# The opening of a two-layer backbone kernel: the first modulation group computed by halves

## The reference, cut to what matters

```python
def reference(x, c, ctx, c_ctx, w_mod, b_mod, g_pre1, ..., w_in, ...):
    for l in range(DEPTH):
        mod = silu(c) @ w_mod[l] + b_mod[l]          # 1024 -> 6 * 1024
        mod_c = silu(c_ctx) @ w_mod[l] + b_mod[l]
        sh1, sc1, gt1, sh2, sc2, gt2 = split(mod, 6)
        h  = rmsnorm(x,  g_pre1[l]) * (1 + sc1)  + sh1
        hc = rmsnorm(xc, g_pre1[l]) * (1 + scc1) + shc1
        y, y_c = token_mixers(h, hc, w_in[l], ...)   # MLA, neighbourhood attention, mLSTM
        x = x + gt1 * rmsnorm(y, g_post1[l])
        h2 = rmsnorm(x, g_pre2[l]) * (1 + sc2) + sh2
        x = x + gt2 * rmsnorm(expert_choice_ffn(h2, w_router[l], w_e1[l], w_e3[l], w_e2[l]), g_post2[l])
        # the same for the context in layer 0
```

## Time and profile before

| | us |
|---|---|
| median of 3 executions | 1842.19 |
| lowest, highest | 1840.27, 1844.49 |
| the profiled execution's own time | 1842.94 |
| its span (first to last instruction) | 1841.2 |
| PE busy, share of the span | 1616.7, 88% |
| DVE busy | 640.7, 35% |
| HBM read | 525.84 MB, 286 GB/s over the span |

### The profile page before, as it was taken

How to read it: one execution, slowest core, us unless ns; L and a number is a source line. 1 busy time by engine, 2 the same in 40 slices (tenths; PEclk the granted TensorE clock), 3 DMA queues, 4 the chain that set the end, 5 groups by cost and what they waited for, 6 DMA issues and landing times.

```text
span 1841.2 us, 23320 instructions
## 1 busy us (share of the span) xinstructions
PE 1616.7 (88%) x9663; PEld 927.2 (50%) x9663; DVE 640.7 (35%) x1196; ACT 345.7 (19%) x878; POOL 258.3 (14%) x275
## 2 busy tenths in 40 slices
PE   6999999999999989989898899999988667675766
PEld 2656466677785423324222477778975223232222
DVE  3665345577744112122020425357422111110101
ACT  3123344111132100100001422442230000000001
POOL 5002221344211000000000001326500000000000
PEclk9999999999999999999999999999999877687778
DMA  9525005264686999999999433247887999999996
GB/s 369 199 69 169 1 1 184 91 220 159 237 316 256 421 421 421 422 421 420 422 421 421 176 106 91 64 141 246 277 342 326 420 421 420 421 421 420 421 422 282
DMA packets 132052, 528.44 MB, mean 287 GB/s; under 512 B 9966, under 2 KB 74644, under 8 KB 76396
## 3 DMA queue, kind: packets, MB, share of 16 engines
q1 hardware_dynamic: 129260, 523.64, 71.8%
q0 software_dynamic: 2688, 3.32, 0.9%
HBM read 525.84 MB, written 1.07 MB: 286 GB/s over the span
## 4 chain that ended last, share of the span: by engine, by line
PE 61%; DMA 32%; DVE 4%; issue 2%; ACT 1%; SPq 0%; DVEq 0%; ACTq 0%
DMA ring<-in_w_e_dram 31%; PE ps L974 14%; PE ps L1280 11%; PE ps L1554 9%; PE ps L1389 5%; PE ps L1333 4%; PE ps L1580 4%; PE ps L886 2%; PE ps L1487 2%; PE ps L1117 2%; PE ps L1211 2%; PE ps L1515 1%; PE ps L1233 1%; DMA ring<-in_w_mod_dram 1%; PE ps L1522 1%
## 5 line engine op out<-in xcount | busy, mean ns | idle before, releaser
L1554 PE MATMUL ps<-ring,arena 128*32 128x256 f32 (+1 forms) x2840 | 376.8, 509 | 100.8 <-DMA ring<-in_w_e_dram 96.9
L1554 PEld LDWEIGHTS ps<-ring,arena 128*32 128x32 f32 (+1 forms) x2840 | 123.8, 129 | 334.3 <-issue 160.0
L1580 PE MATMUL ps<-ring,arena 128*32 128x256 f32 (+1 forms) x1488 | 204.9, 533 | 66.8 <-DMA ring<-in_w_e_dram 65.4
L974 PE MATMUL ps<-arena,ring 128*128 128x512 f32 (+1 forms) x464 | 169.0, 520 | 0.0
L1580 PEld LDWEIGHTS ps<-ring,arena 128*32 128x32 f32 (+1 forms) x1488 | 66.5, 134 | 201.7 <-issue 100.8
L2505 DVE COPY arena<-ps 32x512 f32<-32x512 f32 (+1 forms) x124 | 68.6, 553 | 275.7 <-PE ps L1580 274.4
L1635 ACT ACTIVATE arena<-ps 128x256 f32<-128x256 f32 (+5 forms) x236 | 101.2, 437 | 297.5 <-PE ps L1280 171.5
L1952 ACT ACTIVATE arena<-ps 128x512 f32<-128x512 f32 (+1 forms) x32 | 15.7, 491 | 721.5 <-PE ps L1554 721.5
L2498 DVE TENSOR_TENSOR arena<-arena,ps 128x512 f32<-128x512 f32 (+1 forms) x32 | 17.7, 554 | 369.7 <-PE ps L1554 369.7
L2041 DVE SCALAR_TENSOR_TENSOR arena<-ring,cT,arena 128x2048 f32<-128x2048 f32 x49 | 127.7, 2640 | 10.5 <-DMA ring<-in_w_mod_dram 9.7
L974 PEld LDWEIGHTS ps<-arena,ring 128*128 128x128 f32 x464 | 86.8, 190 | 74.8 <-issue 71.0
(11 more groups left out here) (259 smaller groups left out, 1778.7 us busy)
## 6 DMA issues: line engine op xcount, KB each, us to landing
ring<-in_w_e_dram SPq DMA_DIRECT2D x362, 1024.0 KB, 15.3
ring<-in_w_in_dram SPq DMA_DIRECT2D x44, 1024.0 KB, 10.0
ring<-in_w_mod_dram SPq DMA_DIRECT2D x40, 1024.0 KB, 9.2
arena<-in_w_e_dram SPq DMA_DIRECT2D x17, 1024.0 KB, 7.4
ring<-in_w_out_dram SPq DMA_DIRECT2D x8, 1024.0 KB, 10.7
arena<-in_w_mod_dram SPq DMA_DIRECT2D x8, 1024.0 KB, 13.2
arena<-in_w_br_ml_dram SPq DMA_DIRECT2D x8, 512.0 KB, 7.0
ring<-maxima SPq DMA_DIRECT2D x2, 1024.0 KB, 6.3
```

Source lines behind the costliest of these rows:

```text
L974: mm = pe.matmul(o(ps[:, PROJECTION_BANK[i], :]), a, b, start=k == 0, stop=k == len(pairs) - 1)
L1554: mm = pe.matmul(ps[M * j:M * j + M, m, 0:NW], XSTs[l][e // GROUP % 2][:, kk, e % GROUP, 0:M], w[:, k, j * NW:(j + 1) * NW], start=kk == 0 ...
L1580: mm = pe.matmul(ps[M * j:M * j + M, 3, 0:NW], lhs, w[:, k, j * NW:(j + 1) * NW], start=kk == 0, stop=kk == KD - 1)
```

## The change

Four things.

1. Group 0 of layer 0 is loaded and multiplied in two halves (`q`): row block k of half q holds 512 of the 1024 shift columns and the matching 512 of the scale columns (0.5 MB instead of 1 MB, 16 pieces instead of 8). Half 0 modulates the row blocks 0 to 3 of `hT`, half 1 the blocks 4 to 7. The bias and gain rows are loaded in the matching order (six small transfers on POOL instead of four). The tokens are turned a token block at a time between the products, and copied to `hT` with 512 columns an instruction.
2. The weights of MQ and MK leave the ring: both are loaded between the two halves into places of their own (`first_mq`, `held`). The four projections mq0, mq1, mk0, mk1 run together, row block after row block, in four banks (`first_projections`), with the products of half 1 behind the row blocks 0 to 2, the gate parts behind block 4 and the gate rows behind block 5. The turned gate rows move behind the first half of the values.
3. Of group 1, block 2 moves behind the first half of the value weights and blocks 3, 4 and 5 behind the second half, in the order of the loads. Blocks 6 and 7 stay behind NQ. DVE's own list of sums is not edited.
4. `keep_clock(n, b)` issues n matmuls of 128 columns whose results nobody reads: eight of them between the first products, three before the first projections, and in layer 1 five after the first token block's rows are turned and five after the logits.

```diff
-FIRST_SUMMED = [(0, 1), (2,), (3,), (4, 5), (6, 7), (), ()]
+FIRST_SUMMED = [(0, 1), (), (2,), (3, 4, 5), (6, 7), (), ()]
...
-    loads = [("mod", *MOD_GROUPS[0], k) for k in range(KD)] if layer == 0 else []
+    loads = [("modcols", q, k) for q in range(2) for k in range(KD)] if layer == 0 else []
     for c, ks in zip((C_MQ, C_MK, C_MV, C_MV + BLK, C_NQ, C_NK, C_NV), FIRST_SUMMED):
         if c in (C_NQ, C_NV):
             loads.append(("max", layer, int(c == C_NV)))
-        loads.append(("in", layer, c, BLK))
+        if layer or c not in (C_MQ, C_MK):
+            loads.append(("in", layer, c, BLK))
...
+                    elif kind == "modcols":
+                        q, k = lw, a[0]
+                        if q == 1 and k == 0:
+                            for w, col in ((first_mq, C_MQ), (held, C_MK)):
+                                sp.dma_start(w[:, :].rearrange("p (k n) -> p k n", k=KD),
+                                             w_in[0, :, col:col + BLK].rearrange("(k p) n -> p k n", p=P)).then_inc(sem(f"first_landed_{col}"), 16)
+                        load(n, w_slot(n)[:, 0:D].rearrange("p (v n) -> p v n", v=2),
+                             w_mod[0, k * P:(k + 1) * P, 0:2 * D].rearrange("p (v q n) -> p v q n", v=2, q=2)[:, :, q])
...
+            def keep_clock(n, b):
+
+                for _ in range(n):
+                    pe.matmul(ps[:, b, 0:P], ident[:, :], ident[:, :], start=True, stop=True)
+
+            def first_mod(q, k):
+
+                w = next_slot()[:, 0:D].rearrange("p (j n) -> p j n", j=4)
                 for j in range(4):
-                    mm = pe.matmul(ps[32 * j:32 * j + 32, 6, :], cT[:, k, :], w[:, 512 * j:512 * j + 512],
-                                   start=k == 0, stop=k == KD - 1, skip_group_check=True)
+                    mm = pe.matmul(ps[32 * j:32 * j + 32, 5 + q, 0:256], cT[:, k, :], w[:, j, :], start=k == 0, stop=k == KD - 1,
+                                   skip_group_check=True)
                 mm.then_inc(used, 1)
...
+            def first_mod_turn(q):
+
+                pe.wait_ge(sem(FIRST_DONE[q] + "mod_row"), 1)
+                if q:
+                    pe.wait_ge(sem("first_mod_col"), 1)
+                for i in range(2):
+                    b = 2 * q + i
+                    mm = transpose(ps[:, 7, 128 * i:128 * i + 128], mod_tmp[:, 128 * b:128 * b + 128], P)
+                mm.then_inc(sem(FIRST_DONE[q] + "mod_tr"), 1)
...
-            def first_turn():
-
-                pe.wait_ge(sem("n1_xn"), 4)
-                for k in range(KD):
-                    if k >= 2:
-                        pe.wait_ge(sem("raw_lat"), k - 1)
-                        pe.wait_ge(sem("raw_ctx"), k - 1)
-                    for t in range(4):
-                        mm = transpose(ps[:, 2 * (t // 2) + k % 2, (t % 2) * P:(t % 2 + 1) * P], xn1[:, t, k * P:(k + 1) * P], P)
+            def first_turn(t):
+
+                pe.wait_ge(sem("n1_xn"), t + 1)
+                for b in range(2):
+                    if t >= 2:
+                        pe.wait_ge(sem("raw_ctx"), 2 * (t - 2) + b + 1)
+                    for i in range(4):
+                        mm = transpose(ps[:, 2 * (t % 2) + b, P * i:P * i + P], xn1[:, t, (4 * b + i) * P:(4 * b + i + 1) * P], P)
                     mm.then_inc(sem("n1_tr"), 1)
...
-                    for k in range(KD // 2):
-                        mod_product(0, k)
-                    first_turn()
-                    for k in range(KD // 2, KD):
-                        mod_product(0, k)
-                    mod_turn(0)
+                    for t, ks in enumerate(((0, 1), (2, 3), (4, 5), (6, 7))):
+                        for k in ks:
+                            first_mod(0, k)
+                            if k in (0, 1, 2, 4):
+                                keep_clock(2, 6)
+                        first_turn(t)
+                    first_mod_turn(0)
+                    keep_clock(3, 6)
...
+                def first_rows(k, names):
+
+                    for name in names:
+                        w, col = (first_mq, C_MQ) if name[:2] == "mq" else (held, C_MK)
+                        pe.wait_ge(sem(f"first_landed_{col}"), 16)
+                        j = int(name[2])
+                        mm = pe.matmul(ps[:, PROJECTION_BANK[pj_index(0, name)], :], w[:, :].rearrange("p (k n) -> p k n", k=KD)[:, k, j * P:(j + 1) * P],
+                                       hT[:, k, :], start=k == 0, stop=k == KD - 1, skip_group_check=True)
+                        if k == KD - 1:
+                            assert pj[0] == pj_index(0, name)
+                            pj[0] += 1
+                            mm.then_inc(sem("proj_ready"), 1)
+
+                def first_projections():
+
                     for k in range(KD):
                         pe.wait_ge(sem("n1_lat"), k + 1)
                         pe.wait_ge(sem("n1_ctx"), k + 1)
-                        mm = pe.matmul(ps[:, PROJECTION_BANK[pj_index(0, "mq0")], :], w[:, k, 0:P], hT[:, k, :],
-                                       start=k == 0, stop=k == KD - 1)
-                    mm.then_inc(sem("proj_ready"), 1)
+                        first_rows(k, ("mq0", "mq1"))
+                        if k == 3:
+                            first_mod_turn(1)
+                        first_rows(k, ("mk0", "mk1"))
+                        if k < 3:
+                            for b in ((0, 1), (2, 3, 4, 5), (6, 7))[k]:
+                                first_mod(1, b)
+                        if k == 4:
+                            pe.wait_ge(sem("n1_lat"), KD)
+                            pe.wait_ge(sem("n1_ctx"), KD)
+                            parts_of("gate_parts", lambda k: mgw[:, k, :])
+                        if k == 5:
+                            gate_rows()
...
+                    first_projections()
+                    first_mods(0)
                 else:
+                    w = blk(next_slot())
                     parts_of("gate_parts", lambda k: mgw[:, k, :])
                     feature_major(l, "mq0", w, 0, tq, False)
-                pe.wait_ge(sem("proj_taken"), pj_index(l, "gate_parts") + 1)
-                project(l, "gate_rows", lambda b: b[:, :], [(gate_sum.rearrange("p f d h -> p (f d h)"), gate_parts)])
-                feature_major(l, "mq1", w, 1, tq, True)
-                if l == 0:
-                    first_mods(0)
-                w = blk(next_slot())
-                for j in range(2):
-                    feature_major(l, f"mk{j}", w, j, slice(0, T), j == 1)
+                    gate_rows()
+                    feature_major(l, "mq1", w, 1, tq, True)
+                    w = blk(next_slot())
+                    for j in range(2):
+                        feature_major(l, f"mk{j}", w, j, slice(0, T), j == 1)
...
+                    if l == 0 and half == 0:
+                        rows_turn()
...
+                    if l and j == 0:
+                        pe.wait_ge(sem("shift_taken"), l + 1)
+                        keep_clock(5, 7)
...
                 logit_sums(last)
-                if l == 0:
+                if l:
+                    keep_clock(5, 7)
+                else:
...
+                    for t in range(2, 4):
+                        for b in range(2):
+                            act.wait_ge(sem("n1_tr"), 2 * t + b + 1)
+                            copy(hT[:, 4 * b:4 * b + 4, t * P:(t + 1) * P],
+                                 ps[:, 2 * (t % 2) + b, :].rearrange("p (k n) -> p k n", k=4)).then_inc(sem("raw_lat"), 1)
+                    act.wait_ge(sem("raw_ctx"), 4)
+                    for q in range(2):
+                        act.wait_ge(sem(FIRST_DONE[q] + "mod_tr"), 1)
+                        for b in range(2):
+                            src = ps[:, 7, P * b:P * b + P].rearrange("p (v h r) -> p v h r", v=2, h=2)[:, :, :, 0:2]
+                            ins = copy(modT[:, 0, 0, b:4:2, q:4:2, :].rearrange("p h v r -> p v h r"), src)
+                        ins.then_inc(sem(FIRST_DONE[q] + "mod_col"), 1)
+                        act.wait_ge(sem(FIRST_DONE[q] + "mod_col"), 1)
+                        for k in HALVES[q]:
+                            v = hT[:, k, 0:CTX]
+                            act.activation(v, v, ACT.Identity, bias=mod_col(0, SH1, k, 0), scale=mod_col(0, SC1, k, 0))\
+                                .then_inc(sem("n1_ctx"), 1)
...
+            def first_mod_row(q):
+
+                cols = slice(256 * q, 256 * q + 256)
+                dve.wait_ge(used, KD * q + KD)
+                dve.wait_ge(sem("mod_rows_ready"), 1)
+                own(dve.tensor_tensor(mod_tmp[:, cols], ps[:, 5 + q, 0:256], b_row[:, cols], ALU.add))
+                dve.scalar_tensor_tensor(out=mod_tmp[:, cols], in0=mod_tmp[:, cols], scalar=one_add[:, 0:1], in1=g_row[:, cols],
+                                         op0=ALU.add, op1=ALU.mult).then_inc(sem(FIRST_DONE[q] + "mod_row"), 1)
...
```

(56 more changed lines are left out.)

60 lines of the change are left out of this document (18 added, 42 removed).

## The result

The changed kernel takes 1850.82 us, the median of 4 runs (1849.78 to 1852.66), beside 1843.03 us for the kernel before (4 runs, 1840.27 to 1844.49). The ratio is 1.0037, 95% interval [1.0019, 1.0055]. It is slower, by about 7 us, between 3.5 and 10, by the ratio. The forecast was 1843.5 with a range up to 1848.5, so the time lies outside it, in the direction to which the forecast had given 26 of 100.

What follows compares the result with a forecast made beforehand. The opening was taken as bound by transfers, then PE as the bound. First values +0.9, clock +1.6 and layer 1 -1.15 made +1.35 us, forecast 1843.5 us, with an 8-in-10 range of 1838.5 to 1848.5.

Steps and rivals of the forecast that it cites:

- Half 1 is no wait: Opening: 12.6 MB plus 0.7 of others in by about 36 us, so PE loses nothing waiting for half 1.
- The gain of the opening: First projections end at 59.5 instead of 67.7 us, a gain of 8.2 us, bounds 5 to 9.
- the start S: Opening: start of the first projections, put at 24.8 us, between 24 and 26.
- the work behind it: PE's work from S to the end of the first projections, summed to 34.7 us.
- Half-wide rows stream worse: Rival on the opening's loads: 2 KB runs lower the rate, 9.0 MB in 1 us later, 1844.5; 0.09 together with weak fillers.
- S + 13: Opening: when half 1's last two products are wanted, behind the third row block.
- The order of loads: Group 1's block 7 waits for the second values' slot, PE waits 9 us, first values at 107.5 against 106.6: +0.9.
- Clock: Behind PE's 9 us pause before the first values: half clock costs +1.6 us, bounds 0 and 1.7.
- Layer 1's fillers: Layer 1's routing: fillers keep the clock, -1.15 us, bounds -2.5 and +0.5.
- they hold nothing: Rival on layer 1's fillers: -1.15 becomes 0 to +0.5, 1845; chance 0.09 together with slow rows.
- the gain stays: Faster rival: block 7 does not hold the first values back, they come at 98.4, 1832.8; chance 0.13.
- slow opening: Slower rival: half clock in the opening, S = 26 and slow first projections, 1846.5, or 1849 without full clock before S; chance 0.20.

Runs made afterwards that it cites:

- e8: The change with e2's order, each piece of half 1 loading 64 columns instead of 1024 (modulation of row blocks 4 to 7 wrong): 1837.46 us, ratio 0.9967.
- e6: The change with each 512 KB half piece read as one run of 4 KB a row instead of two of 2 KB: 1850.41 us, ratio 1.0032.
- e9: The change with e2's order and half 1's products placed later, 1, 3 and 4 blocks instead of 2, 4 and 2: 1838.80 us, ratio 0.9974.
- e2: The change with group 1's block 3 loaded ahead of the second half of the values again, beside block 2: 1841.03 us, ratio 0.9986.
- e4: The change with 38 filler matmuls on PE behind nq0, in its pause before the first values: 1848.48 us, ratio 1.0021.
- e7: The change without the eleven fillers of its opening: 1852.25 us, ratio 1.0034.
- e1: The kernel before with only group 1's block 3 loaded behind the second half of the values, beside blocks 4 and 5: 1854.18 us, ratio 1.0052.
- e3: The kernel before with only layer 1's ten fillers added, five in each of two places in the routing: 1843.06 us, ratio 0.9994.
- e5: The kernel before with group 0's 1 MB pieces read as four runs of 2 KB a row instead of one of 8 KB: 1845.63 us, ratio 1.0009.

## Why the prediction was wrong, by its own steps

**The step that failed** is in the opening: "Half 1 is no wait: 12.6 MB plus 0.7 of others is in by about 36 us". The gain of the opening was put at 8.2 us and is 67.70 - 64.10 = 3.6. The 4.6 us that are missing lie in three terms of the opening:

- waits for half 1, forecast 0, measured 2.6 (e8 against the change). The forecast looked at the last two products only. PE waited at block 1, which landed at 31.7, and at block 5, wanted at 37.6 (35.99 + 1.63, the end of the three blocks before it) and landed at 38.3. Block 7 landed at 41.0, not at 36. Of these 5 us half is the rate and half the traffic of others: the step took the rate from the earlier trace rows, where group 0 comes in 8 KB runs, and 13.3 MB at 371 GB/s is 36 us, at the 347 of the change 38; and by 41.0 some 347 x 41 = 14.2 MB had moved, 1.6 beside the 12.6 and not 0.7.
- the start S, forecast 24.8 (24 to 26), measured 26.16. About 1 us of it is slow passes up to 16.7 (e6 and e9, with fast ones from 14.6 and 14.7, start at 25.02 and 25.24).
- the work behind it, forecast 34.7, measured 35.3.

The three are not independent. With half 1 as it is loaded, e2, e4 and e7 start up to 0.8 us sooner and end within 0.3 of the change; only e8, with half 1's loads gone, shows the start and the work by themselves: 61.67 for 59.5.

The mechanism had been named, as the rival *Half-wide rows stream worse*, and priced at 1 us. Its yardstick was right in size: 375 for 410 GB/s is 9% (the 410 is not in the earlier trace rows; the windows from 5 to 15 us have 414 and 411; that the 1 KB runs are what lowered it no run shows), and 371 to 339 over 35 us is 9% too. But it was charged to the 4.2 MB of half 0 only. Half 1 has the same rows and was left at the old rate; at 339 its 13.3 MB are in at 39 us, later than the S + 13 = 37.8 at which they were wanted. The waits in the middle of the projections can't be made up later, as everything behind is in order on PE.

**The order of loads** was right to a tenth: SP issues block 7 with NK at nq0's start + 1.1, and the first values follow nq0's start (95.94) by 16.16 us where 16.2 was forecast. All of the error at the first values (112.10 for 107.5) is that of the opening. e1 shows the step by itself, e2 its absence.

**Clock** behind the pause: forecast +1.6, bounds 0 and 1.7; measured +2.0 (4.21 for 2.23), and e4 takes it away. The bounds were too narrow, since they came from half clock at the first projection, where only part of the stretch was slow (in the traces of e3 and e5 mq0 took 9.86 and 10.03, so one execution is a thin base for a bound). For the opening the forecast counted no slow clock because of the fillers; the passes up to 16.7 were slow all the same, and the 1 us at S is their price, which the end of the projections did not feel.

**Layer 1's fillers**: forecast -1.15, measured -1.4, by the very steps named: keep_busy in 5.32 us for 7.01, the second turning in 1.41 for 1.98, and PE now waits 0.97 us for DVE. The rival that they hold nothing falls by e3's trace.

**The rivals.** That the gain stays is refuted for the change, and e2 shows the condition under which it would. The *slow opening* came by half, as its own middle case had it (S = 26, measured 26.16): a turned token block took 1.91 us where the rival has 1.8, eight passes of the products 1.08, and from 16.7 on all ran fast. Its other half, slow first projections, did not come (four passes in 1.96). But the 1.4 us at S are not what made the kernel slower, since the end of the projections hangs on half 1. The Trainium skill's rule in "TensorE: Matmul & The Clock Gate", Part 4 (PE-mode transpose), by which transposes don't count as activity the way matmuls do, would have kept the opening slow to the first projections. In e7 the turnings ran at 1.09 us for eight from 18.48 on, and the first projections started fast. Thin products stood between the turnings, though, so the rule is not tested by itself.

The sum, term by term: opening and order +0.9 forecast, +5.5 measured; clock +1.6 and +2.0; layer 1 -1.15 and -1.4; stretches not in the forecast 0 and +0.7; together +1.35 and +6.8.

## What to carry to other kernels

In a ring of buffers a load's issue time belongs to the piece that frees its slot: recount the slots whenever one load changes its place, because here one index in a tuple decided 11 us and turned a gain into a loss. When a load is cut into finer columns, take its rate from rows with the same run length, and charge it to every transfer of that shape, not only to the first that is wanted. Then place the consumers by the landings measured, and not by those hoped for: e9 moved the products of three blocks and had 1.7 us for nothing. And where a column of the profile says full clock, compare equal passes early and late before believing it.

## What the runs showed of the hardware

- Loads of the same matrix ran at 351, 341 and 330 GB/s (to 20 us) with runs of 8, 4 and 2 KB, at a DMA share that didn't fall. The share of busy time doesn't show this loss; only the bytes do.
- After a pause of 9.10 us the granted clock was 0.50, still so in the window from 113 to 114, and 20 passes took 4.21 us; with matmuls on the identity in the pause it was 1.00 and they took 2.50.
- In the opening of e7 eight turnings took 1.97 us at 14.72 and 1.09 at 18.48, both in windows whose granted clock reads 1.00: before its first fall the column did not show the slow level, the durations did.
- With thin products between them, turnings ran at the fast 1.09 without any filler (e7 from 18.48).
